# Another order of the VectorE and ScalarE work in the eight mLSTM heads

## The chip, the cores and the metric

The kernel runs on one core of one Trainium2 chip. The metric is the time of one execution on the device in microseconds (us). Inside a core, TensorE (PE) multiplies, VectorE (DVE) and ScalarE (ACT) do elementwise work, and SyncE (SP) and ScalarE issue the DMAs. Each engine works through its own instructions in the order in which they are written, and the engines wait for each other by semaphores.

## What is computed

The reference passes a sequence of 512 tokens of width 1024 through a two-layer transformer block (with a second stream of 256 context tokens), then through a second block of two layers: a convolution and recurrence mixer with a gated feed-forward, and an mLSTM mixer with a gated feed-forward. The change touches the mLSTM mixer alone. Its heads, 8 of them with q and k of width 64 and v of width 128, compute in the reference, chunk by chunk:

```python
log_d = b[..., :, None] - b[..., None, :] + ic[..., None, :]
log_d = jnp.where(causal, log_d, -jnp.inf)
m_row = jnp.maximum(log_inter, jnp.max(log_d, axis=-1))
d_w = jnp.exp(log_d - m_row[..., None])
scores = jnp.einsum('bhjd,bhsd->bhjs', qc, kc) * d_w
num = jnp.einsum('bhjs,bhsv->bhjv', scores, vc) + inter_w[..., None] * jnp.einsum('bhjd,bhdv->bhjv', qc, c_state)
den = jnp.sum(scores, axis=-1) + inter_w * jnp.einsum('bhjd,bhd->bhj', qc, n_state)
h = num / jnp.maximum(jnp.abs(den), jnp.exp(-m_row))[..., None]
```

The kernel computes the same function over all 512 tokens at once: transposed scores of a head, times exponential weights under a causal mask, times v, over the larger of the absolute sum and a threshold `exp(-m)`.

## The kernel before

**Weights.** All weight matrices come as a stream of tiles of 128 x 1024 numbers (512 KB). SyncE loads a tile into one of four buffers `raw`; ScalarE rounds it to `w_hi` (`split`, line 873); VectorE computes the rest `w_lo = raw - w_hi` (`lower_w`, line 2493); TensorE multiplies high by high, high by low and low by high (`three`, lines 1632 to 1634). `split(c)` and `lower_w(c)` work on the tile three behind c (`LEAD = 3`), and a load waits until `lower_w` has freed its buffer.

**The mLSTM stage.** Each head h goes through four key blocks n = 0 to 3 of 128 keys; block n has the queries from 128n on: 512, 384, 256, 128 columns. The turn k = 4h + n of the three engines:

- TensorE (`mlstm`, from line 2275): `score_t` multiplies the q and k of one head for one block (lines 2318, 2319), two turns ahead of its use. `fill` runs the matmuls of the next weight tiles in between, 48 matmuls of 512 columns a head; these tiles give the output gates and v. `values(h, n)` multiplies v by the weights of the turn and sums them (three matmuls at lines 1632 to 1634 and two at 2337 and 2338). Turn n = 1 has `total(h - 1)`, eight matmuls of one column (line 2345), just ahead of `values(h, 1)`; turn 3 has `v_turned(h + 1)`, eight small transposes (line 2286). `score_t(h + 1, 0)` stands in turn (h, 2), behind the first three fill matmuls.
- VectorE (from line 3396): `diagonal` (line 3313) adds the causal mask to the diagonal 128 x 128 block of a gate row, for the exponentials two turns ahead; `weights` (line 3407) multiplies scores by exponentials for the next turn; `lower_part` (line 3414) makes the low part of that product, which `values` waits for. In turn 0 stand `numerator(h - 1)` (lines 3421, 3422, 3425), which divides up the head before, and `denominator(h - 1)` (lines 3429, 3431); in turn 1 `query_key_parts(h + 1)` makes the low parts of the next head's q and k (lines 3302, 3303), which `score_t(h + 1, 0)` waits for; in turns 0 and 2 the fill has `lower_w`; in turn 3 `v_lower`.
- ScalarE (from line 1205): `upper_part` (line 1217) rounds the product of `weights` to its high part; `exponentials` (lines 1124, 1126) takes the diagonal block, for which it waits for `diagonal`, and the rest of a row; `query_key_parts` (line 1118) makes four high parts of the next head's q and k; `fill(h, n)` is a `split` in turns 0 and 2 and the read of a filled bank in turns 1 and 3 (lines 1246, 1249); `threshold_sent` (line 1139) and `row_sent` (line 1133) issue DMAs of 2 KB and of a gate row to all 128 partitions (256 KB); `numerator_square` (line 1224) squares the sums of the head before.

**What sets the order.** All of it is written out by hand: the loop over h and n in each engine's program is the order in which that engine runs. No planner is involved. Per turn before the change ScalarE has `upper_part`, `exponentials`, then (n = 0) the four q and k parts, then the fill; VectorE has `weights` of the next turn, the numerator (n = 0), the diagonal, `lower_part`, the denominator (n = 0), the q and k parts (n = 1), the fill.

**Waits that matter here.** `exponentials` waits for its diagonal, `upper_part` for its `weights`, `lower_part` for its `upper_part`, `lower_w` for its `split`, and `values(h, n)` for `lower_part(h, n)`. `score_t` waits for both q and k parts of VectorE. `numerator` waits for the threshold, its `diagonal` for the gate row (n = 0).

Of the kernel before, what the change touches and what calls it, by code (L numbers as in the profile page):

```python
# [18 lines left out]
HEAD = 64  # L19
N_HEADS = 8  # L20
# [361 lines left out]
def build(nc, ws, vecs, mats, ropes, x_in, ctx_in, bv_in, out, upto=None):  # L382
# [5 lines left out]
    with ExitStack() as stack:  # L388
# [473 lines left out]
        def _(act):  # L862
# [246 lines left out]
                    g = scr[:, pos // 2 % 2, :]  # L1109
                    nc.scalar.activation(g, g, ACT.Silu).then_inc(evac, 1)  # L1110

            def query_key_parts(h):
                b, lo0 = 4 * (h % 2), h % 2 * HEAD
                s, other = slice(lo0, lo0 + HEAD), slice(HEAD - lo0, P - lo0)
                q, k = z[s, h // 2, :], z[s, 4 + h // 2, :]
                for o, src, scale in ((kv[s, b, :], q, 1.0), (kv[other, b, :], q, 1.0),
                                      (kv[s, b + 2, :], k, HEAD ** -0.5), (kv[0:HEAD, b + 3, :], k, HEAD ** -0.5)):
                    nc.scalar.activation(o, src, ACT.Copy, scale=scale).then_inc(s_qk_hi, 1)

            def exponentials(h, n):  # L1120
                act.wait_ge(s_diag, C.next(s_diag))
                j = n * P
                a_col, e = small[:, n * 8 + h:n * 8 + h + 1], scr[:, n % 2, :]
                nc.scalar.activation(e[:, j:j + P], e[:, j:j + P], ACT.Exp, bias=a_col).then_inc(s_exp, 1)
                if n < 3:
                    nc.scalar.activation(e[:, j + P:], row_of(h)[:, j + P:], ACT.Exp, bias=a_col)\
                        .then_inc(s_exp, 1)

            def row_sent(h):

                if h == 7:
                    act.wait_ge(s_gated, 1)
                act.dma_start(row_of(h), row[0][h:h + 1, :].unsqueeze(1).to_broadcast([1, P, SEQ])).then_inc(s_row_at[h % 2], 16)
# [67 lines left out]
            def step(ins):  # L1201
                ins.then_inc(act_own, 1)
                act.wait_ge(act_own, C.next(act_own))

            def mlstm(first):


                prod0 = C.now(s_prod)

                def upper_part(n):  # L1210
                    act.wait_ge(s_prod, C.next(s_prod))
                    k = C.now(s_prod) - prod0 - 1
                    if k >= 2:

                        act.wait_ge(s_pv, C.now(s_pv) + k - 1)
                    j = slice(n * P, SEQ)
                    nc.scalar.activation(kv[:, 8 + 2 * (k % 2), j], scr[:, 2 + k % 2, j], ACT.Copy).then_inc(s_prod_hi, 1)

                def numerator_square(h):
                    act.wait_ge(s_pv, C.now(s_pv) + 4 * (h + 1))  # L1220
                    if h >= 2:

                        act.wait_ge(s_total, h - 1)
                    nc.scalar.activation(xv[:, h % 2, :], ring[:, 2, :], ACT.Square).then_inc(s_on, 1)

                def roots(a, b):
                    act.wait_ge(s_total, b)
                    nc.scalar.activation(small[:, 32 + 4 * a:32 + 4 * b], bank[1][:, 4 * a:4 * b], ACT.Sqrt, scale=4.0 / P)\
                        .then_inc(root_ready, 1)

                def v_upper(h):
                    act.wait_ge(s_turned, C.next(s_turned))
                    nc.scalar.activation(v_parts(h_hi, h), turned_bank(h).rearrange("p (t d) -> p t d", d=P), ACT.Copy)\
                        .then_inc(hi_ready, 1)

                def fill(h, n):
                    if h == 7 and n > 1:
                        return
                    t = 2 * h + n // 2
                    c = first + t  # L1240
                    if n % 2 == 0:
                        split(c)
                        return
                    done(c)
                    if t % 2 or h == 7:
                        nc.scalar.activation(z[:, 8 + h, :], fill_bank(h, 1), ACT.Tanh, bias=o_bias[:, h:h + 1],
                                             scale=0.5).then_inc(s_gate_read, 1)
                    else:
                        nc.scalar.activation(z[:, 15, :], fill_bank(h, 0), ACT.Identity, bias=v_bias[:, h + 1:h + 2])\
                            .then_inc(s_gate_read, 1)  # L1250
                    if n == 3:
                        v_upper(h + 1)

                for h in range(N_HEADS):
                    for n in range(4):
                        if n == 0 and h:
                            numerator_square(h - 1)
                        if n == 2 and h + 2 < N_HEADS:
                            row_sent(h + 2)
                        upper_part(n)  # L1260
                        if h + n == 0:
                            v_upper(0)
                        if n < 2:
                            exponentials(h, n + 2)
                        elif h + 1 < N_HEADS:
                            exponentials(h + 1, n - 2)
                        if n == 0 and h + 1 < N_HEADS:
                            query_key_parts(h + 1)
                        if n == 1 and not h:
                            step(nc.scalar.activation(row[1], row[1], ACT.Exp))  # L1270
                        if n == 1:
                            threshold_sent(h)
                        fill(h, n)
                root_table()
                roots(0, N_HEADS - 1)
                numerator_square(N_HEADS - 1)
                C.next(s_pv, 4 * N_HEADS)
                for h in range(N_HEADS):
                    act.wait_ge(s_normed, h + 1)
                    nc.scalar.activation(y_hi[:, h, :], head_out(h), ACT.Copy).then_inc(hi_ready, 1)  # L1280
                    if h == 1:
                        roots(N_HEADS - 1, N_HEADS)
# [1179 lines left out]
        def _(dve):  # L2462
# [933 lines left out]
            def mlstm(first):  # L3396
# [50 lines left out]
                weights(0, 0)  # L3447
                for k in range(4 * N_HEADS):
                    h, n = divmod(k, 4)
                    if k + 1 < 4 * N_HEADS:  # L3450
                        weights((k + 1) // 4, (k + 1) % 4)
                    if n == 0 and h:
                        numerator(h - 1)
                    if k + 2 < 4 * N_HEADS:
                        diagonal((k + 2) // 4, (k + 2) % 4, prod0)
                    lower_part(h, n)
                    if k == 0:
                        v_lower(0)
                    if n == 0 and h:
                        denominator(h - 1)  # L3460
                    if n == 1 and h + 1 < N_HEADS:
                        query_key_parts(h + 1)
                    fill(h, n)
# [127 lines left out]
```

## Time and profile before

| | |
|---|---|
| median of 3 runs | 3372.53 us (3370.08 to 3374.48) |
| the profiled execution, its own time | 3373.99 us |
| its span, first to last instruction | 3372.2 us |
| TensorE matmul, busy | 3239.4 us, 96% of the span |
| TensorE weight loads, busy | 2691.7 us, 80% |
| VectorE, busy | 2101.3 us, 62% |
| ScalarE, busy | 1212.1 us, 36% |
| mean granted TensorE clock | 0.973 |

The busy times are of different engines beside each other and don't add up. A matmul's end in the trace is modelled, and matmuls overlap, so the distance of their starts tells the pace. A granted clock of 1.00 is 2.4 GHz, 0.50 is 1.2 GHz. The idle time in brackets is that of the engine just before an instruction, with what ended it. The mLSTM heads are at 2765 to 2925 us; line numbers, as L1632, are those of the kernel before.

### The profile page before, as it was taken

Reading aid. Unit: us, or ns where it says so; the run is one execution under the profiler, and the core shown is the slowest. Engines: PE = TensorE matmul, PEld = TensorE weight load, DVE = VectorE, ACT = ScalarE, POOL = GpSimd, SP = SyncE. Lnnn points to the kernel's source line nnn. Section 1 sums busy time; section 2 is a strip of 40 time slices with the busy share of each in tenths; the row PEclk is TensorE's granted clock in tenths of the full one; section 3 lists DMA queues with packets and bytes.
Section 4 is the critical chain, followed back from the end, with each engine's and each line's share of the span. In section 5 each row is a group of like instructions: output and inputs, shape, how many; then the busy total and the mean of one; then the engine's idle time right before and its main releaser. Section 6 shows DMA issues by size and latency. Waiting matters only on the chain.

```text
span 3372.2 us, 42710 instructions
## 1 busy us (share of the span) xinstructions
PE 3239.4 (96%) x16050; PEld 2691.7 (80%) x16050; DVE 2101.3 (62%) x2914; ACT 1212.1 (36%) x1783; POOL 0.2 (0%) x4
## 2 busy tenths in 40 slices
PE   8989999999999999999999999999999998999998
PEld 5878997787878887877778888787888777778886
DVE  4777885655577777656475555765544675555446
ACT  3654434454222223344332222534222265442221
POOL 0000000000000000000000000000000000000000
PEclk8999999999999999999999999999999998999999
DMA  7554552111334553211222232222222345222222
GB/s 242 189 194 150 181 182 86 63 50 63 113 119 144 166 196 100 87 57 51 74 76 100 93 100 93 75 94 82 95 99 94 106 71 63 48 88 100 95 95 74
DMA packets 100715, 358.24 MB, mean 106 GB/s; under 512 B 11208, under 2 KB 12368, under 8 KB 100560
## 3 DMA queue, kind: packets, MB, share of 16 engines
q1 hardware_dynamic: 98864, 352.92, 31.4%
q10 hardware_dynamic: 1696, 3.16, 1.9%
q8 instruction: 108, 1.77, 0.2%
q14 instruction: 47, 0.39, 0.0%
HBM read 351.83 MB, written 2.10 MB: 105 GB/s over the span
## 4 chain that ended last, share of the span: by engine, by line
PE 88%; DVE 6%; ACT 3%; issue 1%; DMA 1%; SPq 0%; DVEq 0%; ACTq 0%
PE ring L1632 25%; PE ring L1633 25%; PE ring L1634 25%; PE bank L1632 2%; PE bank L1633 2%; PE bank L1634 2%; ACT w_hi L873 1%; DVE w_lo L2493 1%; DVE h_lo L2557 1%; DVE scr L2549 1%; PE ring L1936 1%; PE ring L1906 1%; PE ring L1935 1%; PE bank L1960 1%; PE bank L1961 1%
## 5 line engine op out<-in xcount | busy, mean ns | idle before, releaser
L1632 PE MATMUL ring<-h_hi,w_hi 128*128 128x512 f32 (+1 forms) x2776 | 1039.5, 374 | 39.5 <-DVE h_lo L2557 22.5
L1633 PE MATMUL ring<-h_lo,w_hi 128*128 128x512 f32 (+1 forms) x2776 | 1026.4, 370 | 0.0
L1634 PE MATMUL ring<-h_hi,w_lo 128*128 128x512 f32 (+1 forms) x2776 | 1024.9, 369 | 0.0
L2493 DVE TENSOR_TENSOR w_lo<-raw,w_hi 128x1024 fp32r<-128x1024 f32 x598 | 731.2, 1225 | 353.1 <-ACT w_hi L873 335.8
L873 ACT ACTIVATE w_hi<-raw 128x1024 fp32r<-128x1024 f32 x598 | 630.0, 1055 | 722.1 <-PE ring L1634 672.6
L1632 PEld LDWEIGHTS ring<-h_hi,w_hi 128*128 128x128 f32 x2776 | 531.6, 191 | 150.0 <-issue 38.0
L1634 PEld LDWEIGHTS ring<-h_hi,w_lo 128*128 128x128 f32 x2776 | 532.7, 192 | 87.8
L1633 PEld LDWEIGHTS ring<-h_lo,w_hi 128*128 128x128 f32 x2776 | 533.4, 192 | 81.5
L1632 PE MATMUL ring<-y_hi,w_hi 128*128 128x512 f32 (+1 forms) x1456 | 541.2, 372 | 10.2 <-DVE z L2772 7.6
L1633 PE MATMUL ring<-y_lo,w_hi 128*128 128x512 f32 (+1 forms) x1456 | 537.1, 369 | 0.0
L1634 PE MATMUL ring<-y_hi,w_lo 128*128 128x512 f32 (+1 forms) x1456 | 536.6, 369 | 0.0
L1632 PEld LDWEIGHTS ring<-y_hi,w_hi 128*128 128x128 f32 x1456 | 276.4, 190 | 60.2 <-DVE z L2772 10.1
L1634 PEld LDWEIGHTS ring<-y_hi,w_lo 128*128 128x128 f32 x1456 | 276.4, 190 | 46.1
L1633 PEld LDWEIGHTS ring<-y_lo,w_hi 128*128 128x128 f32 x1456 | 276.5, 190 | 44.5 <-issue 0.5
L1549 ACT ACTIVATE scr<-ring 128x512 f32<-128x512 f32 (+1 forms) x96 | 50.5, 527 | 311.3 <-PE ring L1634 311.3
L2988 DVE TENSOR_TENSOR z<-scr 128x512 f32<-128x512 f32 (+1 forms) x96 | 57.9, 603 | 130.0 <-ACT scr L1549 130.0
L2913 DVE SCALAR_TENSOR_TENSOR x<-ring,mod,x 128x512 f32<-128x512 f32 (+1 forms) x80 | 60.1, 751 | 120.3 <-PE ring L1634 120.3
L2804 DVE TENSOR_TENSOR y_lo<-z,y_hi 128x512 fp32r<-128x512 f32 (+1 forms) x112 | 72.3, 647 | 63.1 <-ACT y_hi L1460 62.9
L2794 DVE TENSOR_REDUCE mx<-ring 128x1 f32<-128x768 f32 (+1 forms) x80 | 67.9, 849 | 61.7 <-PE ring L1936 61.1
L1110 ACT ACTIVATE scr<-scr 128x512 f32<-128x512 f32 x40 | 25.3, 632 | 196.3 <-DVE scr L3281 196.3
L1460 ACT ACTIVATE y_hi<-bank 128x512 fp32r<-128x512 f32 (+1 forms) x112 | 63.3, 565 | 75.1 <-PE bank L1634 74.1
L1453 ACT ACTIVATE z<-bank 128x512 f32<-128x512 f32 (+1 forms) x112 | 63.6, 568 | 60.4 <-PE bank L1961 54.8
(367 smaller groups left out, 3090.2 us busy)
## 6 DMA issues: line engine op xcount, KB each, us to landing
raw<-ws SPq DMA_DIRECT2D x614, 512.0 KB, 3.3
z<-ws SPq DMA_DIRECT2D x48, 512.0 KB, 4.4
x<-x_t SPq DMA_DIRECT2D x1, 2048.0 KB, 11.3
out_t<-x SPq DMA_DIRECT2D x8, 256.0 KB, 2.0
z<-xc ACTq DMA_DIRECT2D x6, 256.0 KB, 11.4
xc<-ctx_t SPq DMA_DIRECT2D x1, 1024.0 KB, 8.9
z<-ropes ACTq DMA_DIRECT2D x2, 512.0 KB, 5.0
xc<-xc ACTq DMA_DIRECT2D x2, 256.0 KB, 11.2
```

The costliest lines, as they stand in the source:

```text
L873: nc.scalar.activation(w_hi[:, t % R, :], raw[:, t % R, :], ACT.Copy).then_inc(w_hi_ready, 1)
L1453: nc.scalar.activation(z[:, 13 + k % 2, :T], bank[k % 2][:, :T], ACT.Exp, scale=HEAD ** -0.5)\
L1460: nc.scalar.activation(y_hi[:, 4 + k % 2, :T], bank[k % 2][:, :T], ACT.Exp, scale=HEAD ** -0.5)\
L1549: nc.scalar.activation(scr[:, u % 2, :T], ring[:, c % R, :T], ACT.Relu).then_inc(evac, 1)
L1632: nc.tensor.matmul(o, a_hi, b_hi, start=start, stop=False)
L1633: nc.tensor.matmul(o, a_hi, b_lo, start=False, stop=False)
L1634: return nc.tensor.matmul(o, a_lo, b_hi, start=False, stop=stop)
L2493: nc.vector.tensor_tensor(w_lo[:, u, :], raw[:, u, :], f(w_hi[:, u, :]), ALU.subtract).then_inc(w_ready, 1)
L2794: nc.vector.reduce_max(mx[:, h % 2, qt:qt + 1], view[:, 0:n_kt * P], AX_X).then_inc(s_max, 1)
L2804: nc.vector.tensor_tensor(y_lo[:, b, :T], src, f(y_hi[:, b, :T]), ALU.subtract).then_inc(s_p, 1)
L2913: step(nc.vector.scalar_tensor_tensor(o, ring[:, c % R, :T], g, o, ALU.mult, ALU.add), post)
L2988: step(nc.vector.tensor_tensor(z[:, m % 2, :T], scr[:, m % 2, :T], scr[:, m % 2, :T], ALU.mult))
```

## The change

The same instructions are issued in another order on VectorE and ScalarE, within the mLSTM heads. On ScalarE, turn (h, 0) has the fill's `split` directly behind `upper_part(h, 0)`, then two of the four q and k parts of the next head, then the exponentials of (h, 2); turn (h, 1) has `upper_part(h, 1)`, the other two q and k parts, and the exponentials of (h, 3). For that, `query_key_parts` takes a range of parts. On VectorE, the diagonal stands ahead of the numerator of the head before, and in turn n = 1 `lower_part` is moved to the front, ahead of `weights`, diagonal and the q and k parts. TensorE and SyncE are as before.

```diff
-            def query_key_parts(h):
+            def query_key_parts(h, first=0, last=4):
                 b, lo0 = 4 * (h % 2), h % 2 * HEAD
                 s, other = slice(lo0, lo0 + HEAD), slice(HEAD - lo0, P - lo0)
                 q, k = z[s, h // 2, :], z[s, 4 + h // 2, :]
-                for o, src, scale in ((kv[s, b, :], q, 1.0), (kv[other, b, :], q, 1.0),
-                                      (kv[s, b + 2, :], k, HEAD ** -0.5), (kv[0:HEAD, b + 3, :], k, HEAD ** -0.5)):
+                parts = ((kv[s, b, :], q, 1.0), (kv[other, b, :], q, 1.0),
+                         (kv[s, b + 2, :], k, HEAD ** -0.5), (kv[0:HEAD, b + 3, :], k, HEAD ** -0.5))
+                for o, src, scale in parts[first:last]:
                     nc.scalar.activation(o, src, ACT.Copy, scale=scale).then_inc(s_qk_hi, 1)
...
                 for h in range(N_HEADS):
-                    for n in range(4):
-                        if n == 0 and h:
-                            numerator_square(h - 1)
-                        if n == 2 and h + 2 < N_HEADS:
-                            row_sent(h + 2)
-                        upper_part(n)
-                        if h + n == 0:
-                            v_upper(0)
-                        if n < 2:
-                            exponentials(h, n + 2)
-                        elif h + 1 < N_HEADS:
-                            exponentials(h + 1, n - 2)
-                        if n == 0 and h + 1 < N_HEADS:
-                            query_key_parts(h + 1)
-                        if n == 1 and not h:
-                            step(nc.scalar.activation(row[1], row[1], ACT.Exp))
-                        if n == 1:
-                            threshold_sent(h)
-                        fill(h, n)
+                    more = h + 1 < N_HEADS
+                    if h:
+                        numerator_square(h - 1)
+                    upper_part(0)
+                    if not h:
+                        v_upper(0)
+                    fill(h, 0)
+                    if more:
+                        query_key_parts(h + 1, 0, 2)
+                    exponentials(h, 2)
+                    upper_part(1)
+                    if more:
+                        query_key_parts(h + 1, 2, 4)
+                    exponentials(h, 3)
+                    if not h:
+                        step(nc.scalar.activation(row[1], row[1], ACT.Exp))
+                    threshold_sent(h)
+                    fill(h, 1)
+                    if h + 2 < N_HEADS:
+                        row_sent(h + 2)
+                    upper_part(2)
+                    if more:
+                        exponentials(h + 1, 0)
+                    fill(h, 2)
+                    upper_part(3)
+                    if more:
+                        exponentials(h + 1, 1)
+                    fill(h, 3)
...
                 for k in range(4 * N_HEADS):
                     h, n = divmod(k, 4)
+                    if n == 1:
+                        lower_part(h, n)
                     if k + 1 < 4 * N_HEADS:
                         weights((k + 1) // 4, (k + 1) % 4)
+                    if k + 2 < 4 * N_HEADS:
+                        diagonal((k + 2) // 4, (k + 2) % 4, prod0)
                     if n == 0 and h:
                         numerator(h - 1)
-                    if k + 2 < 4 * N_HEADS:
-                        diagonal((k + 2) // 4, (k + 2) % 4, prod0)
-                    lower_part(h, n)
+                    if n != 1:
+                        lower_part(h, n)
```

## Rows read from the trace of the kernel before

**Rows 1.** The page's first part: busy us, share of the span, instructions.

```profile
PE 3239.4 (96%) x16050; PEld 2691.7 (80%) x16050; DVE 2101.3 (62%) x2914; ACT 1212.1 (36%) x1783; POOL 0.2 (0%) x4
```

**Rows 2.** Waits at 2765 to 2926 us, TensorE: us in total, times, longest.

```profile
PE ring L1632 <- DVE kv L3414: 15.1, 8, 2.4
```

**Rows 3.** Timeline of TensorE, heads 2 and 3: start, us, what [idle before].

```profile
2811.27 0.47 PE L1632 MATMUL ring<-kv,h_hi 128*128 128x512 f32 x1
...
2814.10 0.95 PE L2345 MATMUL bank<-mat,xc 128*128 128x1 f32 x8
2817.40 0.41 PE L1632 MATMUL ring<-kv,h_hi 128*128 128x384 f32 x1 [2.35 <-DVE kv L3414]
...
2818.61 0.63 PE L1632 MATMUL ring<-y_hi,w_hi 128*128 128x512 f32 x1
2819.03 0.63 PE L1633 MATMUL ring<-y_lo,w_hi 128*128 128x512 f32 x1
...
2822.45 0.40 PE L1632 MATMUL ring<-y_hi,w_hi 128*128 128x512 f32 x1
2822.68 0.39 PE L1633 MATMUL ring<-y_lo,w_hi 128*128 128x512 f32 x1
...
2838.37 0.55 PE L1632 MATMUL ring<-kv,h_hi 128*128 128x384 f32 x1 [1.96 <-DVE kv L3414]
```

**Rows 4.** Timeline of ScalarE, head 2, turns 0 and 1.

```profile
2807.53 0.63 ACT L1217 ACTIVATE kv<-scr 128x512 fp32r<-128x512 f32 x1
2810.60 0.40 ACT L1124 ACTIVATE scr<-scr,small 128x128 f32<-128x128 f32 x1 [2.44 <-DVE scr L3313]
...
2811.32 2.59 ACT L1118 ACTIVATE kv<-z 64x512 fp32r<-64x512 f32 x4
2813.93 1.06 ACT L873 ACTIVATE w_hi<-raw 128x1024 fp32r<-128x1024 f32 x1
2814.90 0.51 ACT L1217 ACTIVATE kv<-scr 128x384 fp32r<-128x384 f32 x1
```

**Rows 5.** Timeline of VectorE, head 2, turns 0 and 1.

```profile
2809.68 0.69 DVE L3425 SCALAR_TENSOR_TENSOR z<-z,ring 128x512 f32<-128x512 f32 x1
...
2811.80 0.68 DVE L3431 TENSOR_TENSOR xc<-xc 1x512 f32<-1x512 f32 x1
2815.02 1.23 DVE L2493 TENSOR_TENSOR w_lo<-raw,w_hi 128x1024 fp32r<-128x1024 f32 x1 [2.55 <-ACT w_hi L873]
2816.17 0.42 DVE L3407 TENSOR_TENSOR scr<-ring,scr 128x256 f32<-128x256 f32 x1
...
2816.70 0.55 DVE L3414 TENSOR_TENSOR kv<-scr,kv 128x384 fp32r<-128x384 f32 x1
...
2817.89 0.68 DVE L3303 SCALAR_TENSOR_TENSOR kv<-z,kv 64x512 fp32r<-64x512 f32 x1
```

**Rows 6.** Timeline of TensorE, head 7, turns 1 and 2.

```profile
2921.36 0.95 PE L2345 MATMUL bank<-mat,xc 128*128 128x1 f32 x8
2922.16 0.43 PE L1632 MATMUL ring<-kv,h_hi 128*128 128x384 f32 x1
...
2923.62 0.35 PE L1632 MATMUL ring<-kv,h_hi 128*128 128x256 f32 x1 [0.33 <-DVE kv L3414]
```

**Rows 7.** Timeline of VectorE, head 7: `lower_w` behind `denominator`.

```profile
2919.64 1.21 DVE L2493 TENSOR_TENSOR w_lo<-raw,w_hi 128x1024 fp32r<-128x1024 f32 x1
```

**Rows 8.** DMA issues at 2755 to 2930 us: count, KB each, median us to landing.

```profile
z<-xc ACTq DMA_DIRECT2D x6, 256.0 KB, 11.4
...
xc<-xc ACTq DMA_DIRECT2D x8, 2.0 KB, 3.1
```

**Rows 9.** Windows, TensorE alone: window, us, PE busy, granted clock, DMA share, GB/s.

```profile
2794.70:2801.20 6.50, 6.44 (x17) 0.52 0.92 105
2817.90:2821.70 3.80, 3.80 (x12) 0.55 0.93 135
...
3040.00:3300.00 260.00, 260.00 (x1149) 1.00 0.30 99
```

## The prediction

> **What bounds the kernel now.** The page says that TensorE is busy for 96% of the span [rows 1], so a change pays only where TensorE waits or runs at its lower clock. The changed order stands in one stage, the eight mLSTM heads, at 2765 to 2925 us. I read its waits first: matmuls of L1632 waited for a VectorE result at L3414 (`lower_part`) eight times, 15.1 us in total and up to 2.4 us at once [rows 2]. Then the timeline of head 2, engine by engine.
>
> On TensorE [rows 3] `values(2,0)` starts at 2811.27, eight small matmuls of `total(1)` at 2814.10, and `values(2,1)`, which could follow, starts at 2817.40 after 2.35 us of waiting. Afterwards 512-column matmuls start 0.42 us apart (2818.61, 2819.03), and later 0.23 us apart (2822.45, 2822.68). The same wait stands once in each of heads 0 to 6.
>
> ScalarE [rows 4] shows where it begins: `upper_part(2,0)` ends at 2808.16, then ScalarE sits for 2.44 us until VectorE has written the diagonal of (2,2). Its exponentials start at 2810.60, the four q and k parts of head 3 take 2.59 us from 2811.32, the split of the next weight tile runs from 2813.93 to 2814.99, and `upper_part(2,1)` from 2814.90 to 2815.41. VectorE [rows 5] ends `numerator(1)` at 2810.37 and `denominator(1)` at 2812.48, waits 2.55 us for that split, then runs `lower_w` (2815.02), `weights(2,2)` (2816.17), the diagonal, and `lower_part(2,1)` (2816.70 to 2817.25), which releases TensorE. So the chain is numerator, diagonal, exponentials, four q and k parts, split, `lower_w`, `lower_part`.
>
> **The change on ScalarE.** Nothing is added or removed; instructions change places. The split no longer stands behind the diagonal: it can start when `upper_part(2,0)` ends, 2808.16, and takes 1.06 us [rows 4], to 2809.22. Two q and k parts (half of 2.59, so 1.30) end at 2810.52. The diagonal of (2,2), now ahead of the numerator on VectorE, was written by about 2808.7 (the three instructions of `numerator`, 0.7 us each, ended at 2810.37, so they began near 2808.3, and the diagonal, 0.28 long, now goes there and they follow), so the exponentials wait for nothing and take 0.72 (2810.60 to the start of the next at 2811.32): 2811.24. `upper_part(2,1)`, 0.51 us, ends at 2811.75 instead of 2815.41. The other two q and k parts end at 2813.05. What is late next on ScalarE is the exponential of (2,3), which waits for a diagonal that VectorE reaches near 2814.9; behind it are queued the threshold DMA, the read of the fill's bank and `upper_part(2,2)`. None of them is needed by TensorE before `values(2,2)`, 4 us later.
>
> **The change on VectorE.** Its string up to `denominator(1)` keeps its instructions, and `lower_part(2,0)` keeps its time: the diagonal goes from just behind the numerator to just ahead of it. `lower_w` then starts at 2812.48 without a wait, 1.23 us [rows 5], and `lower_part(2,1)`, now first of its turn, 0.55 us: end 2814.26 at the latest. TensorE can start `values(2,1)` 0.80 us after `total` begins; head 7 shows that distance (2921.36 to 2922.16) [rows 6]. That is 2814.90, 0.6 us later than the operand is ready. Head 7 is the case without q and k parts, and its `lower_w` started at 2919.64 straight behind `denominator` [rows 7]: TensorE did not wait at `values(7,1)`. So the whole wait goes. In all: 15.1 less the 0.33 us of head 7's `values(7,2)` [rows 2, 6] is 14.8 us. The wait is counted from the modelled end of the matmul in front, 0.95 us behind its start and not 0.80, so 0.15 us more for each of seven heads: 1.0 us. Together **15.8 us**.
>
> **What is late next.** The q and k lower parts of head 3 (`score_t(3,0)` waits for both) stand behind this string. Before, `lower_w` to the end of the second took 2815.02 to 2818.57, 3.55 us [rows 5], and the new order holds the same instructions: 2812.48 + 3.55 = 2816.03. The ScalarE parts that they need are there at 2813.05. TensorE reaches `score_t(3,0)` after five matmuls of 384 columns (0.17 each, from 0.23 for 512) and three of 512: 2814.90 + 0.86 + 0.69 = 2816.45. That is 0.4 us in hand, the thinnest place of the new order. I take 0; if the string is longer its bound is the rival below.
>
> **The DMAs that move.** The threshold's 2 KB are sent some 1.5 us earlier (the diagonal of (2,3), which they come behind, is due near 2814.9; before it followed `weights(2,2)`, which began at 2816.17 [rows 5]) and landed 3.1 us after issue; the broadcast of row h+2 landed after 11.4 us [rows 8] and is first read about a head (17 us, below) later. Both stay in the order threshold, row on ScalarE's queue, and neither passes a load of SyncE's. Cost 0; late ones cost only when over 17 us. The weight loads are paced by `lower_w`, four tiles ahead; no split in the stage waited for one, so 0 as well.
>
> **The clock.** After the wait TensorE ran at a mean granted clock of 0.52 over 6.5 us in head 1 and 0.55 over 3.8 us in head 2 [rows 9]: 1.2 GHz, with ends of 2.4 GHz in the windows. There are six such stretches, two long (heads 1 and 4) and four short (2, 3, 5, 6); head 0 has none. At 1.2 GHz stood 2 × 0.48 × 6.5 = 6.2 us in a long and 2 × 0.45 × 3.8 = 3.4 us in a short one, together 2 × 6.2 + 4 × 3.4 = 26 us. Of such time 0.20 in 0.43 is lost (spacing 0.23 against 0.43 [rows 3]): **12.1 us**. In front of each drop TensorE had issued eight one-column matmuls and then waited; a dense stretch of 260 us elsewhere ran at 1.00 throughout [rows 9]. So I take all 12.1 as coming back, with 0 and 12.1 as bounds. Two rules of the Trainium skill read this differently (TensorE: Matmul & The Clock Gate). Its section "What's actually happening" says that the clock is low by default and activity releases it; by that the sum keeps its 12.1 us, and the rows point the same way. Its section "Seeing it yourself" has a peak-current limiter against dense matmuls, but from three busy cores of a die on; were it the cause here, the 12.1 would stay lost. One core runs, and no row shows that limiter's level.
>
> **The tail.** In head 7 nothing is won, and `lower_part(7,1)` now stands ahead of the last diagonal, whose exponential, and behind it `upper_part(7,2)` on ScalarE, was already 0.33 us late for `values(7,2)` [rows 6]. `lower_part` of that width takes 0.55 us [rows 5]. The end of the stage is 0 to 0.6 us later; I take **0.5**, since the chain is already late.
>
> **Sum.** 15.8 + 12.1 - 0.5 = 27.4 us. The profiled execution took 3374.0 us (span 3372.2); minus 27.4 it gives 3346.6. The median of the three runs is 3372.5, 1.5 us lower, and its forecast is 3345. TensorE stays the bound in the stages behind, so nothing is given back. The check from the other side: from `values(2,1)` at 2817.40 to `values(3,1)` at 2838.37, behind a wait of 1.96 [rows 3], are 20.97 us; less 2.1 for that wait and 3.4 × 0.465 = 1.6 for the short stretch, a head without them takes 17.3 us, 4 us less.
>
> **The rivals.** (1) *The clock does not come back*: the waits go, the lower clock stays for as long as now. For it: at least the two long stretches outlast their wait several times. Against: the dense stretch at 1.00. Gain 15.3: 3357 us. (2) *A new wait at `score_t(h+1,0)`*: the string on VectorE is longer than I laid it. For it: only 0.4 us in hand. Against: all its instructions are timed. If it is 1.2 us longer, 0.8 us are lost in each of seven heads, 5.6 us: 3351 us; if 3 us, the wait is as long as the one removed, and all is given back. (3) *Slower*: TensorE without pauses for 150 us is held at 1.2 GHz. Removing the waits gains 15.3 us, and lower-clock time has to grow from 26 us by (15.3 + 6.7) / 0.465 = 47 us, to 73 us, before the kernel is 0.2% slower; over all seven heads (7 × 17.3 = 121 us at full clock) spacing 0.43 for 0.23 would add 105 us: 3450. Only the coincidence of drops with waits speaks against it, and the dense stretch. (4) *The change does not reach the wait*: the split waits for something other than its place in the queue, such as its tile's load, so `lower_w` stays where it is: 3372.5. Against: it started at 2813.93, right behind the q and k parts.
>
> **How the numbers follow.** Forecast 0.79 (3345), rival 1 0.07, rival 2 0.07, rival 3 0.03, rival 4 0.04. A measurement of this kernel can tell about 0.2%, 6.7 us. Faster by more: the forecast and rivals 1 and 2, 0.93; the same: 0.04; slower: 0.03. The runs of before lie 4.4 us apart, and the lower-clock stretches elsewhere may fall differently by some us, so the forecast itself covers 3340 to 3350; with the mild form of rival 2, and some drops that remain, the range is 3340 to 3355. Rival 1's full price, and 3 and 4, are left out of it.
>
> **What would show it.** In the changed profile TensorE should wait for L3414 under 1 us in the whole stage (the tail's), `lower_w` should not wait for the split behind `denominator`, and the clock should be 1.00 from about 2770 to 2898. Heads should be 17.3 us apart. A wait of L2318 (`score_t`) for the q and k parts would be rival 2; clock under 1 with no wait in front, rivals 1 or 3; an unchanged wait for L3414, rival 4. I am wrong above all if ScalarE's parts, halves at 1.30 us, are slower in their new place, or if the clock follows something other than these waits.

## The result

The changed kernel took 3349.0 us (median of 5 runs, 3339.2 to 3354.5), beside 3374.5 us for the kernel before (5 runs, 3370.1 to 3383.7). The ratio is 0.9916, with a 95% interval of 0.9897 to 0.9935 (the quotient of the two medians, 0.9925, lies in it). The forecast was 3345, range 3340 to 3355. The profiled execution took 3349.01 us, its span 3347.2 us, against 3373.99 and 3372.2.

The line numbers move: a few lines are inserted, so `lower_part` is L3424 (L3414 before), `lower_w` L2503, `three` L1642 to L1644, `total` L2355, `score_t` L2328, `upper_part` L1218, the exponentials L1125 and L1127, the q and k parts L1119.

The first part of the page answers [rows 1]: TensorE lost 12.3 us of busy time with the same 16050 matmuls and its weight loads 9.0 us; VectorE and ScalarE are unchanged.

```profile
PE 3227.1 (96%) x16050; PEld 2682.7 (80%) x16050; DVE 2101.3 (63%) x2914; ACT 1212.2 (36%) x1783; POOL 0.2 (0%) x4
```

The waits within the stage (2770 to 2902 us; who waits for what: us in total, times, longest) answer [rows 2]. TensorE's wait for `lower_part` is down from 15.1 us in eight places to 0.8 us in one:

```profile
ACT scr L1125 <- DVE scr L3323: 30.0, 15, 4.5
DVE w_lo L2503 <- ACT w_hi L873: 10.7, 8, 1.6
...
PE ring L1642 <- DVE kv L3424: 0.8, 1, 0.8
```

The timelines of head 2 answer [rows 3], [rows 4] and [rows 5]. First ScalarE: the split (L873) follows `upper_part(2,0)` at once, no exponential waits in turn 0, and `upper_part(2,1)` starts at 2806.30:

```profile
2802.79 0.63 ACT L1218 ACTIVATE kv<-scr 128x512 fp32r<-128x512 f32 x1
2803.31 1.06 ACT L873 ACTIVATE w_hi<-raw 128x1024 fp32r<-128x1024 f32 x1
2804.39 1.29 ACT L1119 ACTIVATE kv<-z 64x512 fp32r<-64x512 f32 x2
2805.70 0.40 ACT L1125 ACTIVATE scr<-scr,small 128x128 f32<-128x128 f32 x1
...
2806.30 0.51 ACT L1218 ACTIVATE kv<-scr 128x384 fp32r<-128x384 f32 x1
2806.84 1.28 ACT L1119 ACTIVATE kv<-z 64x512 fp32r<-64x512 f32 x2
2809.90 0.40 ACT L1125 ACTIVATE scr<-scr,small 128x128 f32<-128x128 f32 x1 [1.78 <-DVE scr L3323]
```

VectorE: `lower_w` has no wait in brackets, and `lower_part(2,1)` comes right behind it:

```profile
2807.05 0.68 DVE L3441 TENSOR_TENSOR xc<-xc 1x512 f32<-1x512 f32 x1
2807.66 1.21 DVE L2503 TENSOR_TENSOR w_lo<-raw,w_hi 128x1024 fp32r<-128x1024 f32 x1
2808.80 0.54 DVE L3424 TENSOR_TENSOR kv<-scr,kv 128x384 fp32r<-128x384 f32 x1
...
2810.51 0.68 DVE L3313 SCALAR_TENSOR_TENSOR kv<-z,kv 64x512 fp32r<-64x512 f32 x1
```

TensorE: `values(2,1)` starts at 2810.17, 0.81 us behind the start of `total`, with no idle time, and the spacing behind it stays at 0.23 us:

```profile
2809.36 0.95 PE L2355 MATMUL bank<-mat,xc 128*128 128x1 f32 x8
2810.17 0.43 PE L1642 MATMUL ring<-kv,h_hi 128*128 128x384 f32 x1
...
2811.13 0.39 PE L1642 MATMUL ring<-y_hi,w_hi 128*128 128x512 f32 x1
2811.36 0.40 PE L1643 MATMUL ring<-y_lo,w_hi 128*128 128x512 f32 x1
2811.59 0.40 PE L1644 MATMUL ring<-y_hi,w_lo 128*128 128x512 f32 x1
2811.83 0.39 PE L2328 MATMUL ring<-kv 128*128 128x512 f32 x1
```

Three windows divide the span at two points, the first `v_upper` (2768.09 before, 2770.32 after) and the first matmul of L2389, now L2399, that spreads the norms behind the heads (2927.30, 2902.34). TensorE alone, window, us, busy, granted clock, DMA share, GB/s; first the kernel before, then the changed one:

```profile
0.00:2768.09 2768.09, 2672.43 (x13455) 0.98 0.34 112
2768.09:2927.30 159.21, 141.71 (x685) 0.91 0.43 63
2927.30:3372.20 444.90, 425.22 (x1912) 0.97 0.26 87
```

```profile
0.00:2770.32 2770.32, 2673.17 (x13455) 0.98 0.34 112
2770.32:2902.34 132.02, 128.76 (x684) 1.00 0.54 76
2902.34:3347.20 444.86, 425.19 (x1912) 0.97 0.26 87
```

I call the middle one the stage. It went from 159.21 to 132.02 us, 27.19 us less, and its clock from 0.91 to 1.00. What stands behind took the same (444.9). What stands ahead took 2.2 us more, with the same code, and that makes 27.2 us in the stage 25.0 us in the pair of profiled executions.

### The profile page after: what moved, and what is told of

The parts are those of the page before. It is cut to its first block, busy times and chain, and to the rows that moved or that the text cites. A ratio compares the mean times of both kernels' runs of the same rounds, so it can differ in the third digit from the quotient of the medians.

```text
span 3347.2 us, 42710 instructions
## 1 busy us (share of the span) xinstructions
PE 3227.1 (96%) x16050; PEld 2682.7 (80%) x16050; DVE 2101.3 (63%) x2914; ACT 1212.2 (36%) x1783; POOL 0.2 (0%) x4
## 4 chain that ended last, share of the span: by engine, by line
PE 90%; DVE 6%; ACT 2%; issue 1%; DMA 1%; DVEq 0%; ACTq 0%; SPq 0%
PE ring L1642 25%; PE ring L1643 25%; PE ring L1644 25%; PE bank L1642 2%; PE bank L1644 2%; PE bank L1643 2%; DVE w_lo L2503 1%; DMA raw<-ws 1%; DVE h_lo L2567 1%; DVE scr L2559 1%; PE ring L1712 1%; ACT w_hi L873 1%; PE ring L1946 1%; PE ring L1945 1%; PE bank L1970 1%
## 5 line engine op out<-in xcount | busy, mean ns | idle before, releaser
L1642 PE MATMUL ring<-h_hi,w_hi 128*128 128x512 f32 (+1 forms) x2776 | 1039.2, 374 | 40.0 <-DVE h_lo L2567 22.9
L1644 PE MATMUL ring<-h_hi,w_lo 128*128 128x512 f32 (+1 forms) x2776 | 1025.4, 369 | 0.0
L2503 DVE TENSOR_TENSOR w_lo<-raw,w_hi 128x1024 fp32r<-128x1024 f32 x598 | 731.2, 1225 | 335.6 <-ACT w_hi L873 318.4
L873 ACT ACTIVATE w_hi<-raw 128x1024 fp32r<-128x1024 f32 x598 | 630.5, 1056 | 723.0 <-PE ring L1644 672.8
L1642 PEld LDWEIGHTS ring<-h_hi,w_hi 128*128 128x128 f32 x2776 | 532.1, 192 | 150.5 <-issue 37.9
L1644 PEld LDWEIGHTS ring<-h_hi,w_lo 128*128 128x128 f32 x2776 | 532.6, 192 | 87.1
L1642 PE MATMUL ring<-y_hi,w_hi 128*128 128x512 f32 (+1 forms) x1456 | 539.6, 371 | 10.4 <-DVE z L2782 7.7
L1644 PE MATMUL ring<-y_hi,w_lo 128*128 128x512 f32 (+1 forms) x1456 | 535.8, 368 | 0.0
L1642 PEld LDWEIGHTS ring<-y_hi,w_hi 128*128 128x128 f32 x1456 | 275.5, 189 | 60.3 <-DVE z L2782 10.3
L1644 PEld LDWEIGHTS ring<-y_hi,w_lo 128*128 128x128 f32 x1456 | 275.4, 189 | 45.4
```

Source lines behind the costliest of these rows:

```text
L873: nc.scalar.activation(w_hi[:, t % R, :], raw[:, t % R, :], ACT.Copy).then_inc(w_hi_ready, 1)
L1642: nc.tensor.matmul(o, a_hi, b_hi, start=start, stop=False)
L1644: return nc.tensor.matmul(o, a_lo, b_hi, start=False, stop=stop)
L2503: nc.vector.tensor_tensor(w_lo[:, u, :], raw[:, u, :], f(w_hi[:, u, :]), ALU.subtract).then_inc(w_ready, 1)
```

## The experiments

All were compared by two figures of their traces: the length of the stage, and the distance of two `v_upper` (L1233 or so), which is one head. The heads and the tail repeat to 0.03 us (head 0 can be up to 0.6 us longer by lower clock left over from the stage before: in the split alone, `lower_part` alone, four parts ahead, and the q and k parts computed three times, the granted clock is 0.50 over its first microsecond), while the whole times of one kernel lie up to 17 us apart. In the profiled executions the stage began anywhere from 2766.6 to 2778.8 us, with nothing changed ahead of it, and what stands behind it took 443.4 to 447.8 us. Stages and heads are those of one profiled execution each; the last column has the median of all executions and their number.

| kernel | stage, us | head 0 | heads 1 to 6 | tail from head 7's `v_upper` | whole, us (executions) |
|---|---|---|---|---|---|
| before | 159.21 | 16.22 | 20.94 to 22.61 | 13.50 | 3374.5 (5) |
| changed | 132.02 | 14.17 | 17.31 to 17.32 | 13.97 | 3349.0 (5) |
| ScalarE's part alone | 131.55 | 14.14 | 17.31 to 17.33 | 13.49 | 3347.7 (4) |
| VectorE's part alone | 134.25 | 15.92 | 17.30 to 17.48 | 13.96 | 3353.1 (4) |
| diagonal alone | 135.09 | 16.22 | 17.36 to 17.77 | 13.49 | 3353.2 (1) |
| `lower_part` to the front alone | 151.95 | 15.95 | 19.07 to 20.85 | 13.96 | 3368.5 (1) |
| split ahead alone | 133.17 | 14.98 | 17.31 to 17.59 | 13.49 | 3350.4 (4) |
| four q and k parts ahead | 133.08 | 15.22 | 17.31 to 17.32 | 13.97 | 3348.2 (2) |
| tail put back | 131.61 | 14.16 | 17.32 to 17.33 | 13.50 | 3351.6 (4) |

**ScalarE's part alone.** The kernel before with the changed `query_key_parts` and loop of ScalarE, as in the diff of the change; VectorE's loop stays.

> ScalarE in the new order, VectorE as before. The new kernel's stage, from the first v_upper to the first spread of the normalisation (2770.32 to 2902.34), takes 132.0 us, that of before 159.2. By the steps of the prediction the split is at its early place here too, lower_w starts straight behind denominator, and lower_part(h,1), last of its turn, is ready 1.68 us after it: about 2814.6 in head 2 against 2814.9 at which TensorE comes. Theory 1 (each part alone takes the wait away): TensorE waits under 1 us in all of the stage for L3414, the clock is 1.00 in it, and without the late tail the stage takes 131.5 to 132.5 us. Theory 2 (both parts are needed): the exponentials wait for a diagonal behind numerator, lower_part(h,1) comes 0.5 us or more late in each of seven heads, the stage takes 135 us or more.

The stage took 131.55 us, the heads 17.32 us, and the whole 3347.7 us, ratio 0.992 (0.9902 to 0.9938). Its waits in the stage:

```profile
DVE w_lo L2503 <- ACT w_hi L873: 11.1, 8, 1.6
...
PE ring L1642 <- DVE kv L3424: 0.3, 1, 0.3
```

Theory 1 holds: this part alone gives all of it, and the tail stays as it was.

**VectorE's part alone.** The reverse: ScalarE as before, VectorE's loop as in the change.

> VectorE in the new order, ScalarE as before. The exponentials of (h,2) find their diagonal, so the four q and k parts and the split come 2.0 us earlier (split's end 2813.0 in head 2's terms), lower_w at 2813.0, lower_part(h,1) first of its turn, ready at 2814.7, TensorE at 2814.9. Theory 1 (each part alone takes the wait away): wait for L3414 under 1.5 us in all, at most 0.3 us a head more at score_t for the q and k parts; stage 132 to 134 us. Theory 2 (both needed): 0.5 us or more a head, 135.5 us or more.

The stage took 134.25 us, the whole 3353.1, ratio 0.9928 (0.9909 to 0.9947). Heads 1 to 6 lose 0.17 us or less against the changed kernel. TensorE waited for `lower_part` 2.1 us, more than the 1.5 expected: 0.81 in the tail, and 1.28 in head 0, where `numerator` does not exist and the diagonal's move brings nothing, so that the split stays late. The stage is just above theory 1's 134 us and well under theory 2's 135.5.

```profile
PE ring L1632 <- DVE kv L3414: 2.1, 2, 1.3
...
2785.57 0.41 PE L1632 MATMUL ring<-kv,h_hi 128*128 128x384 f32 x1 [1.28 <-DVE kv L3414]
```

**The two halves of VectorE's part.** First the diagonal alone:

```diff
                     if k + 1 < 4 * N_HEADS:
                         weights((k + 1) // 4, (k + 1) % 4)
+                    if k + 2 < 4 * N_HEADS:
+                        diagonal((k + 2) // 4, (k + 2) % 4, prod0)
                     if n == 0 and h:
                         numerator(h - 1)
-                    if k + 2 < 4 * N_HEADS:
-                        diagonal((k + 2) // 4, (k + 2) % 4, prod0)
                     lower_part(h, n)
```

> Only the diagonal ahead of the numerator on VectorE; lower_part(h,1) stays last of its turn, ScalarE as before. lower_w at 2813.0 in head 2's terms, lower_part ready at 2815.25, TensorE could go at 2814.9: a wait of 0.4 us a head, too short for the clock to fall; stage 132.0 + 7 x 0.45 - 0.5 = 134.7 us. The rival, that any wait behind total's small matmuls brings the lower clock, gives 12 us more: 147.

135.09 us for 134.7 expected, with the clock at 1.00 (one execution). The sum agrees, but it is made up otherwise than expected, by 0.4 us in every head: head 0 keeps a wait of 1.84 us (1.81 before), heads 2, 4 and 6 wait 0.32 us, and heads 1, 3 and 5 not at all:

```profile
2779.89 0.41 PE L1632 MATMUL ring<-kv,h_hi 128*128 128x384 f32 x1 [1.84 <-DVE kv L3414]
...
2815.02 0.41 PE L1632 MATMUL ring<-kv,h_hi 128*128 128x384 f32 x1 [0.32 <-DVE kv L3414]
```

Then `lower_part(h,1)` alone:

```diff
+                    if n == 1:
+                        lower_part(h, n)
                     if k + 1 < 4 * N_HEADS:
                         weights((k + 1) // 4, (k + 1) % 4)
...
-                    lower_part(h, n)
+                    if n != 1:
+                        lower_part(h, n)
```

> Only lower_part(h,1) to the front of its turn, the rest as before. The split stays at 2813.93, lower_part is ready at 2816.7 instead of 2817.25: waits of 1.4 to 1.8 us in place of 1.96 to 2.35, 3.7 us less in all. Theory A (the clock falls for any wait of over a microsecond behind the small matmuls): six stretches of the lower clock as before, stage 159.2 - 3.7 + 0.5 = 156 us. Theory B (it falls only for the longer waits): fewer than six, stage down to 144 us when there are none. I expect between, two to four stretches, 148 to 153 us.

151.95 us, as expected between the theories (one execution). TensorE still waits in every head from 1 to 6, 1.42 to 1.82 us behind `total`:

```profile
PE ring L1632 <- DVE kv L3414: 11.3, 8, 1.8
...
2792.72 0.41 PE L1632 MATMUL ring<-kv,h_hi 128*128 128x384 f32 x1 [1.43 <-DVE kv L3414]
...
2812.19 0.66 PE L1632 MATMUL ring<-kv,h_hi 128*128 128x384 f32 x1 [1.82 <-DVE kv L3414]
```

The stage as a window (us, TensorE busy, granted clock), where the kernel before has 0.91:

```profile
2766.86:2918.81 151.95, 138.22 (x685) 0.94 0.46 64
```

The lower clock came in heads 2 to 6, five times for the two to four expected, and not in head 1, whose wait of 1.43 us is as long as those of heads 3 and 5 that had it. Each stretch is about as long as the four short ones before; the two long ones are gone. So neither theory A nor B is the whole, and one wait may bring a drop while its like does not; what decides between them is not shown.

**Split ahead alone.** On ScalarE of the kernel before, the fill of turn 0 is called ahead of the exponentials:

```diff
                         if h + n == 0:
                             v_upper(0)
+                        if n == 0:
+                            fill(h, 0)
                         if n < 2:
                             exponentials(h, n + 2)
...
-                        fill(h, n)
+                        if n:
+                            fill(h, n)
```

> The kernel before with one edit: ScalarE's split of turn (h,0) directly behind upper_part(h,0); exponentials, four q and k parts and all of VectorE's order as before. In head 2's terms: split's end 2809.2, exponentials from 2810.6 (the diagonal is late as before), four parts to 2813.9, upper_part(h,1) to 2814.4; lower_w runs from 2812.4 and lower_part(h,1) waits for upper_part: ready at 2815.0, TensorE at 2814.9. Theory 1 (the place of the split is what counts): waits for L3414 of at most 0.3 us a head, no lower clock, stage 131.5 to 133.5 us. Theory 2 (diagonal or the halved q and k parts are needed too): 135 us or more.

133.17 us; ratio 0.992 (0.9903 to 0.9937). TensorE waits 0.15 us in heads 2, 4 and 6 and, as before the change, 0.3 us in head 7. This one move carries 26 of the 27 us; head 0 alone has 0.5 us of clock left over from the stage before.

```profile
PE ring L1635 <- DVE kv L3417: 0.8, 4, 0.3
```

**Four parts ahead.** The changed kernel with `query_key_parts(h + 1)` whole where its first half stood, and the second call gone.

> The new kernel with all four q and k parts ahead of the exponentials of (h,2) on ScalarE instead of two. upper_part(h,1) ends 1.3 us later than the new kernel's 2806.81, at 2806.84 + 1.28 = 2808.1, before lower_w lets VectorE take it at 2808.80. Theory 1 (no step of ScalarE between split and upper_part is on the path): stage 132.0 as in the new kernel, within 0.4. Theory 2 (the halving matters): each of seven heads loses some of 1.3 us, 134 us or more.

This execution took 8183 us and can't be used. The granted clock falls to 0.36 near 895 us, but TensorE was slow long before: in the first 880 us it ran 1931 matmuls where the changed kernel ran 5217, and its 256-column matmuls start 0.42 us apart (302.32, 302.74) where the changed kernel's start 0.12 us apart (339.95, 340.07), all at a granted clock that reads 1.00. VectorE's and ScalarE's busy times are near their usual ones (2114.9 and 1222.4 us). So it was TensorE alone, from the start of the execution and in stages that the edit does not touch. Two of its windows:

```profile
0.00:880.00 880.00, 871.57 (x1931) 1.00 0.21 70
...
900.00:1200.00 300.00, 298.88 (x1004) 0.36 0.22 74
```

The same kernel again:

> The kernel with all four q and k parts ahead of the exponentials once more. The first execution took 8183 us at a mean granted clock of 0.442; its clock fell at about a ninth of its span, long before the mLSTM stage, and stayed near a third, so it says nothing of the edit. If that was the chip's state at that moment, this execution takes 3345 to 3355 us with the stage at 132.0 within 0.4 (theory 1) or 134 and more (theory 2). If the edit itself brings it, it takes over 8000 us again.

3348.15 us (two runs, ratio 0.9919, 0.989 to 0.9948), so the edit by itself does not bring that slow execution, whose cause stays open. Heads 1 to 6 take 17.31 to 17.32 us as in the changed kernel: halving the q and k parts gains nothing there. Head 0 is 1.05 us longer, so that the stage lies between the theories. 0.59 us of that stand ahead of `values(0,0)` (3.15 us behind `v_upper` instead of 2.56), beside lower clock left from the stage before (0.62 over its first 1.4 us). The other 0.46 are theory 2 in head 0. With no head before it, VectorE is early there and waits for `upper_part(0,1)`, 2.53 us instead of 1.22, because that now stands behind four parts. `lower_part(0,1)` then ends at 2772.50 and TensorE starts `values(0,1)` at 2772.64; the q and k parts end at 2774.35 and `score_t(1,0)` starts at 2774.45:

```profile
2774.45 0.47 PE L2326 MATMUL ring<-kv 128*128 128x512 f32 x1
```

So halving gains in head 0 alone. In head 2, counted from the start of `upper_part(2,0)`, `upper_part(2,1)` ends after 5.3 us (2800.12 to 2805.45) instead of 4.0 (2802.79 to 2806.81), and no matmul is later for it:

```profile
2800.12 0.63 ACT L1218 ACTIVATE kv<-scr 128x512 fp32r<-128x512 f32 x1
...
2801.72 2.59 ACT L1119 ACTIVATE kv<-z 64x512 fp32r<-64x512 f32 x4
...
2804.94 0.51 ACT L1218 ACTIVATE kv<-scr 128x384 fp32r<-128x384 f32 x1
```

**How much is in hand.** In the changed kernel, `lower_part(h,1)` of heads 0 to 6 computed three times:

```diff
+                    for _ in range(2 if n == 1 and h < N_HEADS - 1 else 0):
+                        step(nc.vector.tensor_tensor(kv[:, b + 1, j], scr[:, 2 + k % 2, j], f(kv[:, b, j]), ALU.subtract))
                     issue(nc.vector.tensor_tensor(kv[:, b + 1, j], scr[:, 2 + k % 2, j], f(kv[:, b, j]), ALU.subtract), s_p)
```

> The new order, with the low part of lower_part(h,1) computed three times instead of once in heads 0 to 6, one after another: 2 x 0.6 = 1.2 us more on VectorE ahead of the operand of values(h,1). The trace of the new kernel has the operand ready at 2809.34 and TensorE's first matmul at 2810.17, 0.8 us in hand. If that distance is the slack, TensorE waits 0.4 to 0.5 us for L3424 in each of seven heads (the line moves by a few), 3.1 us, and the q and k parts, 0.6 us in hand, then cost 0.1 to 0.3 us more: stage 135.5 to 137 us, clock 1.00. If the operand has more room than the rows show, under 133; if less (VectorE's string is fully exposed), 140.

137.31 us, just above the 135.5 to 137 expected (one execution, 3360.0 us), heads of 18.04 instead of 17.32. The two extra take 2815.54 - 2814.38 = 1.16 us, and TensorE starts at 2816.25 instead of 2814.95 + 0.80 = 2815.75:

```profile
2814.38 1.13 DVE L3425 TENSOR_TENSOR kv<-scr,kv 128x384 fp32r<-128x384 f32 x2
2815.54 0.56 DVE L3426 TENSOR_TENSOR kv<-scr,kv 128x384 fp32r<-128x384 f32 x1
```

```profile
2814.95 0.94 PE L2355 MATMUL bank<-mat,xc 128*128 128x1 f32 x8
2816.25 0.41 PE L1642 MATMUL ring<-kv,h_hi 128*128 128x384 f32 x1 [0.35 <-DVE kv L3426]
```

So 1.16 - 0.50 = 0.66 us are in hand at `values(h,1)`. The other 0.2 us of a head are lost at `score_t`. For that place, the first low part of q and k was computed three times:

```diff
+                for _ in range(2 if h else 0):
+                    step(nc.vector.tensor_tensor(kv[0:HEAD, b + 1, :], z[s, h // 2, :], f(kv[s, b, :]), ALU.subtract))
```

> The new order, with the first low part of q and k on VectorE computed three times in heads 1 to 7: 2 x 0.72 = 1.44 us more ahead of score_t(h+1,0) and of weights(h,3). In the new kernel q and k are ready at 2811.19 and TensorE takes them at 2811.83, 0.6 us in hand. So a wait of 0.8 us before score_t in six to seven heads (that of head 1 has it in the stage before in one case), 5 us: stage 137 us, no lower clock. If rival 2 of the prediction were near, the wait would be the full 1.4, stage 142; if score_t has more room, under 134.

139.25 us (one execution, 3354.2 us), heads of 18.30: 0.99 us more a head for 2813.04 - 2811.59 = 1.45 us of extra work, so 0.46 us are in hand. I had expected 137, from 0.64 us between the end of the parts and TensorE's start. Not all of that distance is in hand: the result ends at 2814.33 and the waiting matmul starts 0.10 us later, and the next one stands 0.30 us behind it instead of 0.22. The profile puts the wait down to "issue", not to VectorE, but it moves with VectorE's extra work:

```profile
2811.59 1.41 DVE L3313 TENSOR_TENSOR kv<-z,kv 64x512 fp32r<-64x512 f32 x2
2813.04 0.69 DVE L3314 TENSOR_TENSOR kv<-z,kv 64x512 fp32r<-64x512 f32 x1
2813.65 0.68 DVE L3315 SCALAR_TENSOR_TENSOR kv<-z,kv 64x512 fp32r<-64x512 f32 x1
```

```profile
2814.43 0.47 PE L2328 MATMUL ring<-kv 128*128 128x512 f32 x1 [0.74 <-issue]
2814.73 0.39 PE L2329 MATMUL ring<-kv 128*128 128x512 f32 x1
```

**What brings the lower clock.** In the changed kernel, `total`'s eight matmuls issued four times over in heads 1 to 7, so that TensorE never idles:

```diff
-                    for tt in range(4):
+                    for tt in [*range(4)] * (4 if h < N_HEADS - 1 else 1):
                         m = nc.tensor.matmul(bank[1][:, 4 * h + tt:4 * h + tt + 1],
```

> The new order, with total's eight one-column matmuls issued four times over in heads 1 to 7 (the same sums again, nothing waits for them longer than before): 24 more of 0.1 us each, 2.4 us a head, 7 x 2.4 = 16.8 us, and TensorE never idle. Theory A (the clock falls for lack of columns streamed, be it waiting or one-column matmuls): the lower clock behind each of the seven, 3.4 to 6.8 us long, so 11 to 20 us on top: stage 132.0 + 16.8 + 11 to 20 = 160 to 169 us. Theory B (it falls only when TensorE waits): clock 1.00 in the whole stage, 149 us.

The stage took 165.69 us (one execution, 3383.2 us), 33.7 more than the changed kernel. The 32 matmuls take 3.49 us from their start to the next one's instead of 0.81, so 7 × 2.68 = 18.8 us are their own. The other 14.9 us are lower clock, less the tail's wait of 0.8 us, which is gone here: a mean of 0.90 over 165.7 us is 33 us at 1.2 GHz, and 0.465 of those are 15.

```profile
2772.18:2937.87 165.69, 163.25 (x852) 0.90 0.43 61
```

TensorE waited for nothing before the stage's end, and the spacing still went from 0.23 to 0.43:

```profile
2793.91 3.63 PE L2355 MATMUL bank<-mat,xc 128*128 128x1 f32 x32
2797.40 0.43 PE L1642 MATMUL ring<-kv,h_hi 128*128 128x384 f32 x1
...
2799.12 0.63 PE L1644 MATMUL bank<-y_hi,w_lo 128*128 128x512 f32 x1
2799.54 0.63 PE L2328 MATMUL ring<-kv 128*128 128x512 f32 x1
```

The lower clock came seven times, behind each of the seven groups, with no wait in front. That is theory A and not B: no wait was needed for it here, a run of one-column matmuls was enough.

**The tail put back.** In the changed kernel `lower_part(7,1)` goes last of its turn again:

```diff
-                    if n == 1:
+                    if n == 1 and h + 1 < N_HEADS:
                         lower_part(h, n)
...
-                    if n != 1:
+                    if n != 1 or h + 1 == N_HEADS:
                         lower_part(h, n)
```

> The new order in heads 0 to 6; in head 7 lower_part(7,1) stands last of its turn again, as before the change. The wait for values(7,2), 0.81 us in the new kernel, should be 0.33 again: stage 132.0 - 0.5 = 131.5 us. In the whole time that is not to be told from the new kernel: 0.990 to 0.995 of before. The rival, that the tail is late for another reason (the split's early place on ScalarE), leaves it at 132.0.

131.61 us, the tail 13.50 instead of 13.97: 0.47 us back, the whole time 3351.6 us, ratio 0.9936 (0.9919 to 0.9952), not to be told from the changed kernel. The wait for `values(7,2)` is 0.3 us again:

```profile
PE ring L1642 <- DVE kv L3424: 0.3, 1, 0.3
```

## Why the prediction was right

**The chain.** Shown. The prediction's times for head 2 lie on the measured ones once the 4.75 us by which head 2 begins earlier (its `v_upper` at 2801.81 for 2806.56) are taken off. Split from 2803.41, measured 2803.31. `upper_part(2,1)` ended by 2807.00, measured 2806.81. `lower_w` from 2807.73, measured 2807.66. `lower_part(2,1)` ready at 2809.51, measured 2809.34. `values(2,1)` from 2810.15, measured 2810.17. q and k ready at 2811.28, measured 2811.19; `score_t` from 2811.70, measured 2811.83.

**Waits, 15.8 us, and clock, 12.1 us, less 0.5.** The sum was 27.4, the stage gave 27.19. By the traces behind the table, heads 0 to 6 are 27.66 us shorter. Counted as in the prediction, their waits are 15.9 of it (2.05 in head 0, and 12.91 + 6 × 0.15 in heads 1 to 6), which leaves 11.8 for the clock, and the tail cost 0.47. A head takes 17.32 us for the 17.3 of the check. That the clock's share comes back in full was argued from what stood ahead of each drop. The changed stage ran at 1.00, so it did come back, and rival 3, a dense stage held down, has no sign. The repeated `total` adds that the lower clock also came behind one-column matmuls without a wait.

**What the prediction credited wrongly.** It laid the gain to the early diagonal, the split and `lower_part` at the front together. The experiments say that any one of the first two is nearly enough: the split ahead alone gives 26.0 us, the diagonal alone 24.1, and both meet the same bound, 17.3 us of matmuls a head. They do not add. `lower_part` at the front alone gives 7.3 us, and beside ScalarE's part nothing but the tail's loss. This could have been read ahead: the early diagonal lets the four q and k parts start 2.0 us sooner, and the split behind them ends at 2813.0 for a `lower_w` that can't start before 2812.5.

**Late next.** Both margins look right within 0.06 us, 0.6 at `values(h,1)` for 0.66 measured and 0.4 at `score_t` for 0.46, but by luck: two errors cancel. The prediction took the whole distance from the result to TensorE's start as in hand, of which 0.15 to 0.18 us is not. And it made the distances too short: they are 0.83 and 0.64 us in head 2 where it had 0.64 and 0.42, since the operands were ready 0.17 and 0.09 us earlier than laid out, and `score_t` came 0.13 us later. Rival 2's price holds in kind: with the string 1.45 us longer, 0.99 us were lost in a head.

**The forecast against the median.** 3345 was set on 3372.5, the median of three runs; with five runs it was 3374.5. The measured median of 3349.0 lies 4 us above the forecast, with runs from 3339 to 3354.5: 2 us are that base, the other 2 are within the scatter of the medians. In the traces the scatter is made outside the stage, up to 12 us ahead of it and up to 4.4 us behind it, where nothing was changed; its sources were not followed. The four rivals found no support: the clock came back (against 1), no new wait (against 2), no slower stage (3), and the change reached the wait (against 4).

## What to carry to other kernels

Where one engine waits for a chain through two others, look in each in-order queue for an instruction on the chain that stands behind work which is not on it, and move that one; here the split behind an exponential that waited. Several such moves do not add up: the first that reaches the bound takes the gain, and each later one should be priced against what is left, with its own cost elsewhere (the tail). Price a wait of TensorE with what follows at the lower clock, which here was three quarters as much again (11.8 us for 15.9), and judge small changes by the length of the stage in the trace rather than by whole runs.

## What the runs showed of the hardware

- Thirty-two one-column matmuls in a row, 3.5 us with no idle time, were followed by 1.2 GHz as a wait is: seven times of seven in the stage of the one execution, at a cost of 15 us beside the 18.8 us of the matmuls themselves. A TensorE that the profile shows as busy can still lose its clock.
- A wait of 1.43 us behind `total` was followed by the lower clock in head 5 and not in head 1 (`lower_part` alone), while waits of 1.81 and 1.84 us without `total` ahead of them were not (head 0 of the kernel before and of the diagonal alone).
- From the end of a VectorE result to the start of the matmul that waits for it lie 0.15 us (2816.10 to 2816.25) or 0.10 (2814.33 to 2814.43), which are no slack.
- One execution took 8183 us, the same kernel then 3348 us. TensorE alone was slow, from the start: 1931 matmuls in the first 880 us for 5217. The granted clock read 1.00 there, 0.36 from 895 us on and 0.46 over the last 900 us, so in this execution it did not tell the pace; the distance of the matmuls' starts did.
